# Where the output projection's steps stand in two attention slots, layer norm's statistic three steps later, and four weight halves on GpSimd

## The reference

```python
# first block, per layer
hn = _rmsnorm(h, norm_mix[layer])
o = attention(q, k, v)             # layer 0 stick-breaking, layer 1 dilated
h = h + o @ w_o[layer]
h = h + _swiglu(_rmsnorm(h, norm_ffn[layer]), w_gate[layer], w_up[layer], w_down[layer])
...
# second block
u = causal_dwconv(v_c * sigmoid(gl_c), conv_conf_w) + conv_conf_b
u = silu(layer_norm(u, conf_ln_g, conf_ln_b))
y_b = u @ w_conf_out
mix = (sigmoid(g_a) * y_a + sigmoid(g_b) * y_b) @ w_o
x = x + g1 * mix
```

## Time and profile before

| | us |
|---|---|
| median of 3 runs (2092.49, 2095.94, 2096.28) | 2095.94 |
| the profiled execution | 2094.5 |
| its span, first to last instruction | 2092.7 |
| TensorE busy | 2028.3 (97%) |
| VectorE busy | 1065.9 (51%) |
| ScalarE busy | 827.7 (40%) |
| GpSimd busy | 614.4 (29%) |
| mean granted TensorE clock | 0.991 |

### The profile page before, as it was taken

The page is one execution under the profiler, slowest core; times in us unless marked ns, Lnnn a source line. Parts: engine busy times, 40 slices in busy tenths (PEclk is TensorE's granted clock), DMA queues, the critical chain, the costliest instruction groups (busy, mean ns, idle before and its releaser), DMA issues.

```text
span 2092.7 us, 28539 instructions
## 1 busy us (share of the span) xinstructions
PE 2028.3 (97%) x9356; PEld 1640.2 (78%) x9356; DVE 1065.9 (51%) x1425; ACT 827.7 (40%) x1167; POOL 614.4 (29%) x400
## 2 busy tenths in 40 slices
PE   7999999999998999999999999999999989999997
PEld 5777788888886776788888877888887877888886
DVE  6666544343464666444343454699855543332323
ACT  5455434332252444444342354422226345322224
POOL 1111245341133333246340244444442021001012
PEclk9999999999999999999999999999999999999999
DMA  4212245443333433335443232323332323233332
GB/s 152 70 61 70 91 141 179 143 150 101 91 120 71 91 80 81 101 131 184 149 139 101 90 110 70 99 92 100 94 97 81 100 70 99 92 100 93 97 100 100
DMA packets 62877, 218.71 MB, mean 105 GB/s; under 512 B 7664, under 2 KB 7792, under 8 KB 62704
## 3 DMA queue, kind: packets, MB, share of 16 engines
q1 hardware_dynamic: 59760, 213.96, 32.3%
q0 software_dynamic: 3072, 4.20, 1.5%
HBM read 211.83 MB, written 2.10 MB: 102 GB/s over the span
## 4 chain that ended last, share of the span: by engine, by line
PE 87%; issue 3%; POOL 3%; DVE 3%; ACT 2%; DMA 1%; SPq 0%; POOLq 0%; DVEq 0%; ACTq 0%
PE G L1333 28%; PE G L1334 27%; PE G L1335 27%; POOL qkv L1208 1%; PE Z L1423 1%; PE Z L1442 1%; PE O L1460 1%; ACT wh L341 0%; DVE sp L781 0%; DMA qkv<-tmp 0%; POOL kl L1198 0%; DMA h<-x_t 0%; POOL ql L1198 0%; DVE wl L676 0%; DVE ez L798 0%
## 5 line engine op out<-in xcount | busy, mean ns | idle before, releaser
L341 ACT ACTIVATE wh<-raw 128x1024 fp32r<-128x1024 f32 x348 | 369.0, 1060 | 966.7 <-PE G L1335 960.9
L1333 PE MATMUL G<-xh,wh 128*128 128x512 f32 x1640 | 650.2, 396 | 21.4 <-DVE xl L681 8.4
L1334 PE MATMUL G<-xl,wh 128*128 128x512 f32 x1640 | 642.3, 392 | 0.0
L1335 PE MATMUL G<-xh,wl 128*128 128x512 f32 x1640 | 642.0, 391 | 0.0
L676 DVE TENSOR_TENSOR wl<-raw,wh 128x1024 fp32r<-128x1024 f32 x288 | 400.1, 1389 | 204.8 <-ACT wh L341 201.8
L1333 PE MATMUL G<-yh,wh 128*128 128x512 f32 x960 | 376.5, 392 | 12.2 <-DVE wl L676 5.9
L1333 PEld LDWEIGHTS G<-xh,wh 128*128 128x128 f32 x1640 | 310.2, 189 | 99.0 <-DVE wl L676 15.2
L1334 PE MATMUL G<-yl,wh 128*128 128x512 f32 x960 | 374.6, 390 | 0.0
L1335 PE MATMUL G<-yh,wl 128*128 128x512 f32 x960 | 374.5, 390 | 0.0
L1335 PEld LDWEIGHTS G<-xh,wl 128*128 128x128 f32 x1640 | 310.2, 189 | 66.0
L1334 PEld LDWEIGHTS G<-xl,wh 128*128 128x128 f32 x1640 | 310.5, 189 | 63.5 <-issue 1.0
(11 more groups left out here) (189 smaller groups left out, 1718.0 us busy)
## 6 DMA issues: line engine op xcount, KB each, us to landing
raw<-stream SPq DMA_DIRECT2D x348, 512.0 KB, 3.5
araw<-ada_w SPq DMA_DIRECT2D x48, 512.0 KB, 4.3
qkv<-tmp POOLq DMA_DIRECT2D x64, 64.0 KB, 4.1
h<-x_t SPq DMA_DIRECT2D x8, 256.0 KB, 6.5
out_t<-h SPq DMA_DIRECT2D x8, 256.0 KB, 2.4
con<-const_d SPq DMA_DIRECT2D x1, 1344.0 KB, 10.2
cs<-c_row SPq DMA_DIRECT2D x1, 512.0 KB, 4.2
vec<-vec_d SPq DMA_DIRECT2D x1, 212.0 KB, 3.9
```

The costliest lines, as they stand in the source:

```text
L341: eng.activation(wh[s][:, :, :], raw[s][:, :, :], ACT.Copy).then_inc(w_hi, 1)
L1333: eng.matmul(total[:, :], wh[s][:, k, :], src_h[:, k, :], start=k == 0, stop=False)
L1334: eng.matmul(total[:, :], wh[s][:, k, :], src_l[:, k, :], start=False, stop=False)
L1335: mm = eng.matmul(total[:, :], wl[s][:, k, :], src_h[:, k, :], start=False, stop=k == kt - 1)
```

## The change

Three things. First, `project` in the last slot takes its steps from a table with the slot's marks instead of by proportion. For layer 0 the gaps had 1, 4, 2, 1 and 6 steps and have 1, 7, 2, 1 and 3; for layer 1 they had 2, 5, 1, 1, 5 and have 3, 5, 2, 1, 3. Second, layer norm's `statistic` stands behind all eight steps of the second tile of `U_GB` instead of behind five, and `spread_root` behind five steps of the next tile instead of behind two. Third, the low halves of unit `U_GB + 3` and of `U_CO`, four in all, are made by GpSimd behind its halves of `U_GB + 2`, and no longer by VectorE around `output`; VectorE now waits for the last of them before `mix`.

```diff
+        LAST_FILL = ({0: 0, 2: 1, 10: 8, 13: 10, 15: 11, 24: 14}, {0: 0, 4: 3, 12: 8, 15: 10, 17: 11, 24: 14})
...
-            eng.wait_ge(w_lo, 2 * (U_GB + 3))
-            split_lo(U_GB + 3, 0)
-            for n in range(KD // 2):
+            for n in range(KD):
                 output(n)
-            split_lo(U_GB + 3, 1)
-            for n in range(KD // 2, KD):
-                output(n)
-            split_lo(U_CO, 0)
-            split_lo(U_CO, 1)
+            eng.wait_ge(w_lo, 2 * (U_CO + 1))
             eng.wait_ge(evac[1], U_GB)
...
             split_lo(U_GB + 1, 0)
             inverse_root(S_VAR, 5)
             split_lo(U_GB + 1, 1)
-            for s in range(2):
-                split_lo(U_GB + 2, s)
+            for u in (U_GB + 2, U_GB + 3, U_CO):
+                for s in range(2):
+                    split_lo(u, s)
...
-                            for m in range(lo * 14 // 24, hi * 14 // 24):
+                            for m in range(LAST_FILL[layer][lo], LAST_FILL[layer][hi]):
                                 product(U_WO[layer], m // 7, yh, yl, o_lo, base, ks=[m % 7])
...
             product(U_GB, 0, xh, xl, mod_lo, 0)
-            product(U_GB, 1, xh, xl, mod_lo, 0, ks=range(0, 5))
+            product(U_GB, 1, xh, xl, mod_lo, 0)
             statistic(sq_added, KD * (Q_VAR + 1))
-            product(U_GB, 1, xh, xl, mod_lo, 0, ks=range(5, KD))
             u = U_GB + 1
-            product(u, 0, xh, xl, mod_lo, 0, ks=range(0, 2))
+            product(u, 0, xh, xl, mod_lo, 0, ks=range(0, 5))
             spread_root(S_VAR)
-            product(u, 0, xh, xl, mod_lo, 0, ks=range(2, KD))
+            product(u, 0, xh, xl, mod_lo, 0, ks=range(5, KD))
             product(u, 1, xh, xl, mod_lo, 0)
```

## The result

The changed kernel takes 2081.71 us (median of four runs, 2079.28 to 2082.60), the kernel before 2095.88 (four runs, 2092.49 to 2096.28): ratio 0.9934, 95% interval 0.9917 to 0.9951. It is faster, 14.2 us by these medians, where the forecast was 2086.5 us (9 to 10 us faster) with a range down to 2082.5. The profiled execution took 2082.6 us, its span 2080.8 against 2092.7.

A forecast was written before the change was run, and what follows sets the result against it. TensorE was taken to bound the kernel (87% of the chain); 2.07 + 1.38 + 3.74 + 2.36 = 9.6 us off the profiled 2094.5 gave 2084.9, by the median 2086.3, forecast as 2086.5 us, range 2082.5 to 2090.5.

The forecast's parts named there:

- Part 1: Last slot of layer 0: three more steps fit in TensorE's 2.82 us gap before `turn_weights(0)`, gaining 2.07 us.
- part 2: Last slot of layer 1: one more step each ahead of `scores` and before `turn_weights(1)`, gaining 1.38 us.
- Rival (b): Steps put in the attention gaps fill nothing: 3.45 us less gain, 2090.0 us; chance 0.10.
- Part 3, the wait for `ssum`: Layer norm: three steps moved ahead of the statistic cut TensorE's 2.39 us wait by 2.05 us, leaving 0.34.
- Part 3, the clock: Behind layer norm's statistic: nine matmuls slowed by the low clock regain full clock, gaining 1.69 us.
- Part 4: Four low halves on GpSimd remove TensorE's gap before U_GB + 3, gaining 2.36 us.
- Rival (a): Clock behind the statistic falls anyway, or did not fall in the median's runs: 1.7 us less gain, 2088.2; chance 0.17.
- The port: Port shared by GpSimd and VectorE, an exclusive lock: two `ln_lo` would end about 0.7 us later.
- (c): GpSimd's first half is late, held by VectorE's `ln_lo` or simply long: 0.3 to 1 us, 2087.2; chance 0.13.
- (d): GpSimd sets the pace over the four halves, making the kernel slower than before, 2100.3 us; chance 0.02.
- The base: Starting time of the forecast: median of three runs, 2095.94 us, 1.4 us above the profiled execution.

The follow-up runs named there:

- e2: The changed kernel as it is, run again beside the kernel before on the same chip: 11.0 us below it by the means.
- e11: The changed kernel once more, beside the kernel before on one chip: 10.9 us below it by the means.
- e10: The kernel before plus unread matmuls in three gaps (layer 0's `turn_weights(0)`, second statistic, U_GB + 3): 3.5 us below the kernel before by the means.
- e14: The changed kernel with one more step moved in either layer, statistic one step later, unread matmuls in four other waits: 2077.71 us, ratio 0.9919 to the kernel before.

## Why the prediction was wrong

The step that failed is the price of the clock behind the gaps: 1.69 us at the statistic and nothing at the other two places, where the runs give 3.4 to 3.5 us in all. The first median lies below the range by this and by chance together; the mean of all 14 runs of the changed kernel, 2083.0 us, would lie inside it. By its steps:

- **Part 1 and part 2 (waits).** Right in the first profile: 2.1 and 1.3 us for 2.07 and 1.38, remaining gaps 0.78, 0.24 and 0.65 us, `o_lo` hidden, the waits for the U_WO half unchanged. Rival (b) is out. Not foreseen was that the wait ahead of `scores`, foretold as at most 0.2 us, depends on a transfer that comes 1.1 us later in some executions (e2 and e11).
- **Part 3, the wait for `ssum`.** Right: 0.18 us left of 2.23.
- **Part 3, the clock.** Right was that the low clock behind the statistic goes with the change: none of 11 profiles with the gap shortened or filled has it. Its size rested on one execution: I took the 1.69 us of nine slow matmuls for the whole of it, where other executions of the same code have 3.3 us there, or nothing. What it is worth by itself is not shown; with the gap filled alone it was 0.4 us.
- **Part 4 and the gap of part 1.** Here the sum had no clock term, because the clock behind them was full in that one profile; I even cited the gap before U_GB + 3 as evidence that such gaps leave it full. It fell there in 2 of 9 profiles, and behind layer 0's gap in 5 of 8, at 2.82 us a longer gap than the statistic's. Together the clock behind the three gaps is worth 3.5 us (e10, 0.9 either way), or 11.3 - 7.9 = 3.4 us by the difference from the waits, not 1.7. How it divides among them stays open, since filled alone the statistic's gap gave 0.4 us and layer 0's 0.3. Rival (a) priced the clock only as a loss against the forecast; the same doubt upwards was missing, and with it the low end of the range.
- **GpSimd.** Right in each part: half ready at 1596.16 for 1596.43, none late, `mix` not delayed. The port showed as foretold: two `ln_lo` took 1.32 and 1.15 us in place of 0.69 beside halves on GpSimd, without cost. Rivals (c) and (d) are out.
- **The base.** 2095.94, the median of three runs, lies 1.6 us above the mean of all 113, and the first four runs of the changed kernel 1.7 us below the mean of its 14. The sum from the better base is 2094.4 - 9.6 = 2084.8; the mean of the changed kernel is 2083.0.

So of the 14.2 us, 7.9 are waits, some 3.4 the clock behind them, and some 3 the draw of the first runs, which is luck and no merit of the change. The split between waits and clock is a difference of means; only e10 shows the clock's price by itself, on the kernel before.

## What to carry to other kernels

A gap of the engine that bounds the kernel costs more than its length when the clock falls behind it, and one profile shows this for one execution only. Here the clock fell behind gaps of 2.0 to 2.8 us in some profiles and not in others. So ask of every such gap, not just of the one with slow matmuls behind it, and let the doubt widen the range both ways. Before the last microseconds are counted, take the mean of many runs of the kernel before; here it moved the base by more than some of the terms. Where a wait can't be shortened, matmuls for nothing in it are a cheap test of what the clock costs, if all such waits are filled together; in e14 they also removed most of the scatter, in e10 they did not (standard deviation 1.2 us against 1.3 beside it).

## What was unexpected

- The scatter of the executions goes mostly with TensorE's clock: 1.8 us for each 0.001 of mean clock, and a standard deviation of 0.36 us over five runs once four waits were filled, where it was 1.8. A second source is the transfer for `kl` in layer 1's last slot, which came 1.1 us later in 5 of 18 profiles.
- The same gap in the same code is followed by a full clock in one execution and by 1.2 GHz in the next: behind layer 0's gap of 2.8 us the clock fell in five profiles of eight.
- Filling one gap alone gave 0.3 to 0.5 us for two of them, filling three 3.5 us. Unless the third, never filled alone, is worth nearly all, that is not a sum of the parts, and it is not explained.
